# The second gate/up piece of each expert issued by ScalarE on its own queue

## The reference

```python
def swiglu(x, w_gate, w_up, w_down):
    return (jax.nn.silu(x @ w_gate) * (x @ w_up)) @ w_down

yb = swiglu(x_pad[tok], w_gate_e[e], w_up_e[e], w_down_e[e]).astype(jnp.float32) * w[:, None]
```

## Time and profile before

| | us |
|---|---|
| median of three runs | 1398.07 (1396.43 to 1402.14) |
| the profiled execution | 1402.14 |
| its span in the trace | 1400.4 |
| TensorE busy | 1307.5 (93%) |
| TensorE weight load busy | 973.2 (69%) |
| VectorE busy | 900.2 (64%) |
| ScalarE busy | 706.9 (50%) |
| GpSimd busy | 420.8 (30%) |

### The profile page before, as it was taken

How to read it: one execution, slowest core, us unless ns; L and a number is a source line. 1 busy time by engine, 2 the same in 40 slices (tenths; PEclk the granted TensorE clock), 3 DMA queues, 4 the chain that set the end, 5 groups by cost and what they waited for, 6 DMA issues and landing times.

```text
span 1400.4 us, 15961 instructions
## 1 busy us (share of the span) xinstructions
PE 1307.5 (93%) x6084; PEld 973.2 (69%) x6084; DVE 900.2 (64%) x1167; ACT 706.9 (50%) x863; POOL 420.8 (30%) x266
## 2 busy tenths in 40 slices
PE   7999999999979999989799999999999999999865
PEld 4989886666656776455587777777777777777722
DVE  4001116645666565564388888888888888888858
ACT  4222333333323221012377888887888778887610
POOL 3232312212223342017233333323233333233204
PEclk9999999999999999989999999999999999999978
DMA  4732202111112151430499999999999999999684
GB/s 154 259 102 72 68 20 68 64 39 38 57 38 67 65 203 54 195 132 19 155 387 373 372 365 370 374 366 370 362 373 360 361 365 371 361 363 349 233 368 179
DMA packets 75291, 311.36 MB, mean 222 GB/s; under 512 B 17660, under 2 KB 17788, under 8 KB 57040
## 3 DMA queue, kind: packets, MB, share of 16 engines
q1 hardware_dynamic: 55728, 276.64, 53.8%
q0 software_dynamic: 19488, 33.70, 6.4%
HBM read 305.74 MB, written 42.01 MB: 248 GB/s over the span
## 4 chain that ended last, share of the span: by engine, by line
PE 65%; DMA 21%; DVE 4%; ACT 4%; issue 3%; POOL 3%; POOLq 0%; SPq 0%; DVEq 0%; ACTq 0%
DMA raw<-in_w_gu 19%; PE PS L647 18%; PE PS L891 9%; PE PS L841 5%; PE PS L844 4%; PE PS L838 4%; PE PS L755 4%; PE PS L703 4%; PE PS L773 3%; ACT w_hi_e L1109 3%; PE PS L726 3%; POOL tab_d L1628 2%; PE PS L714 2%; PE PS L675 2%; PE PS L676 2%
## 5 line engine op out<-in xcount | busy, mean ns | idle before, releaser
L1426 DVE TENSOR_TENSOR w_lo_e<-raw,w_hi_e 128x2048 fp32r<-128x2048 f32 x192 | 435.3, 2285 | 14.3 <-ACT w_hi_e L1109 14.0
L1109 ACT ACTIVATE w_hi_e<-raw 128x2048 fp32r<-128x2048 f32 x192 | 368.3, 1919 | 119.8 <-DMA raw<-in_w_gu 75.1
L1642 POOL DMA_INDIRECT y_d<-y_slots,tab x64 | 120.8, 1887 | 412.1 <-ACT y_slots L1141 284.7
L1596 POOL TENSOR_TENSOR w_lo<-ring,w_hi 128x1024 fp32r<-128x1024 f32 x54 | 128.3, 2376 | 327.0 <-ACT w_hi L1016 327.0
L1269 DVE CUSTOM_DVE_ANT_0 region<-PS,region 128x128 f32<-128x128 f32 (+1 forms) x64 | 30.6, 478 | 183.2 <-PE PS L703 181.1
L838 PE MATMUL PS<-w_hi_e,xs_hi 128*128 128x512 f32 x512 | 144.2, 403 | 0.0
L841 PE MATMUL PS<-w_hi_e,xs_lo 128*128 128x512 f32 x512 | 142.8, 401 | 0.0
L844 PE MATMUL PS<-w_lo_e,xs_hi 128*128 128x512 f32 x512 | 137.5, 390 | 0.0
L1060 ACT ACTIVATE region<-region,nmax 128x128 f32<-128x128 f32 (+3 forms) x80 | 43.6, 546 | 150.3 <-DVE nmax L1269 150.0
L841 PEld LDWEIGHTS PS<-w_hi_e,xs_lo 128*128 128x128 f32 x512 | 92.7, 188 | 30.6 <-DVE xs_lo L1452 12.4
L844 PEld LDWEIGHTS PS<-w_lo_e,xs_hi 128*128 128x128 f32 x512 | 96.2, 188 | 20.8
(11 more groups left out here) (182 smaller groups left out, 2154.3 us busy)
## 6 DMA issues: line engine op xcount, KB each, us to landing
raw<-in_w_gu SPq DMA_DIRECT2D x128, 1024.0 KB, 11.3
raw<-in_w_down_e SPq DMA_DIRECT2D x64, 1024.0 KB, 11.0
ring<-in_w_merge SPq DMA_DIRECT2D x32, 640.0 KB, 4.0
parts<-y_d SPq DMA_DIRECT2D x8, 1536.0 KB, 16.2
ring<-in_w_proj SPq DMA_DIRECT2D x22, 512.0 KB, 3.7
region<-in_w_out SPq DMA_DIRECT2D x1, 4096.0 KB, 14.1
parts<-y_d SPq DMA_DIRECT2D x4, 1024.0 KB, 19.9
bias_d<-bias_rows SPq DMA_DIRECT2D x3, 1280.0 KB, 11.7
```

The costliest lines, as they stand in the source:

```text
L1109: nc.scalar.activation(w_hi_e[b][:, lo:hi], raw[b][:, lo:hi], ACT.Copy).then_inc(made, 1)
L1426: nc.vector.tensor_tensor(w_lo_e[b][:, lo:hi], raw[b][:, lo:hi], w_hi_e[b][:, lo:hi].bitcast(F32), ALU.subtract).then_inc(made, 1)
L1596: nc.gpsimd.tensor_tensor(wl, w, wh.bitcast(F32), ALU.subtract).then_inc(w_lo_made, 1)
L1642: pool.indirect_dma_start(y_d, bass.IndirectOffsetOnAxis(ap=rows, axis=0), y_slots[:, b, :], None, bounds_check=last_row, oob_is_err=False ...
```

## The change

The second piece of experts 1 to 63 is no longer issued by SyncE (its wait on `gu_b` goes with it) but by ScalarE, on ScalarE's own queue. It has no wait of its own: it stands behind `make_silu`, which waits for the same `gu_b` count. The second piece of expert 0 stays on SyncE.

```diff
             for e in range(1, N_EXP):
                 sp.wait_ge(gu_a, e + QT - 1)
                 load_first(e)
-                sp.wait_ge(gu_b, e + QT - 1)
-                load_second(e)
                 if e >= 2:
                     sp.wait_ge(y_done, e + QT - 2)
                     load_down(e - 1)
...
+            def load_second(e):
+
+                act.dma_start(raw[e % 2][:, PART:GU], a["w_gu"][e][:, PART:GU]).then_inc(p1_in[e % 2], 16)
+
...
             make_silu(3)
+            load_second(1)
             copy_hT(3)
             high_x(0)
             for e in range(N_EXP):
...
                     high_second(e + 1)
                 make_silu(e + QT)
+                if e + 2 < N_EXP:
+                    load_second(e + 2)
                 high_down(e)
```

## The result

The change makes the kernel slower by 1%: 1412.76 us (median of 4 runs, 1409.14 to 1422.03) against 1397.38 us on the same chip, a ratio of 1.0101, 95% interval 1.0073 to 1.0129. 1398 had been predicted. An unchanged copy of the changed kernel gave 1.0087 later (1.0053 to 1.0121), and a copy of the one before 1.0000.

A forecast was written before the change was run, and what follows sets the result against it. It took the transfers, with DMA engines near their end (share 0.98, 367 GB/s), to set the 10.0 us period. All terms were 0, summing to 0 on the profiled 1402.14 us; against the median it forecast 1398 us, range 1391 to 1405.

The forecast's parts named there:

- What bounds the kernel: Experts' loop: transfers at 367 GB/s set the 10.0 us period, TensorE 7% behind; landing time is the line's length.
- Issue work: 63 issues moved from SyncE to ScalarE: covered by its waiting for pieces, taken as 0, at most 21 us.
- The time of the issue: Second piece on ScalarE: issued 3.3 us later behind the silu, landing in 7.8 us, just when needed; 0.
- SyncE's wait: Down weights on SyncE: now wait only for `y_done`, which comes last anyway; 0, at most 3.6 us gained at the start.
- So the rate stays and with it the period.: Transfers in the loop: the line never runs empty, so the period stays at 10.0 us; main term, 0.
- First piece shares and lands later: First piece's landing: second piece takes turns from it, up to 2.0 us at one expert in three; 1418 us, chance 0.20.
- the faster rival: First piece's landing: comes earlier, so TensorE stops less; 13 us gained, 1385 us, at most 43 us; chance 0.24.
- Gathers late: Gathers: a second busy queue slows them to 15.9 us where 15.7 is allowed; 6 us slower or 1428 us; chance 0.06.
- Same line after all: ScalarE's transfers: join the same line, so only the 3.3 us later issue stays; slower, chance 0.04.

The follow-up runs named there:

- spread: The kernel before, with the slots in use put on even and odd partitions alike: ratio 0.9704, 1359.23 us.
- b_early: The changed kernel with the second piece issued ahead of the rounding of the previous second piece, behind its own wait on `gu_b`: ratio 1.0050, run again 1.0040.
- a_half: The changed kernel with the first piece in two transfers with rows of 4 KB instead of one with 8 KB: ratio 1.0210.
- b_half: The changed kernel with the second piece in two transfers with rows of 4 KB instead of one with 8 KB, on ScalarE: ratio 1.0437.
- before_b_half: The kernel before with the second piece in two transfers with rows of 4 KB, on SyncE's one line: ratio 1.0061.
- a_act: The kernel before with the first piece issued by ScalarE on its own queue, the second staying on SyncE: ratio 1.0108.

## Why the prediction was wrong, by its own steps

- **What bounds the kernel.** Right that the transfers set the pace and that the hop from first piece to copy to down product is where TensorE stops: all of its new idle time came there. Wrong that 367 GB/s was an end, and that a landing is the length of one line: the 8th of 16 increments came after 6.4 us, so the long line was that of half of the parts. A mean share of 0.98 over 16 engines does not say that the next order of the same bytes could not go faster: spread moved them at 395. Both had a share near 1, so a share counts time under way, not rate.
- **Issue work, 0.** Nothing in the runs speaks against it: the same small transfer costs the same from SyncE.
- **The time of the issue.** This step failed. It took the place behind the silu for the time of the silu, so 3.3 us later in every period. The sequencer runs ahead, and the median issue is no later than before. In exchange it can be held by any landing that is waited for ahead of it, here in 22 of 62 periods, which the step didn't look at. b_early against the change shows the price: 0.5%. That the second piece would land in 7.8 us was too low also: 9.3 in the median, 10.2 in the expert shown.
- **SyncE's wait, 0.** Right. At the start the down weights of expert 1 did go at 689.66, right behind the first piece of expert 2 (before: 4.0 us behind it); the next first piece followed that of expert 2 by 6.4 us in both kernels, so it brought nothing.
- **"So the rate stays and with it the period."** This is the main term, put at 60 x (10.0 - 10.0) = 0, and it failed: 10.21 us and 360 GB/s, 12.6 us in the loop. The argument was that a line of three or four pieces never runs empty. It does run thin when the piece that is waited for is not the one being moved: TensorE stops, frees no buffer, and nothing new is issued (a share of 0.87 in the expert of 13.82 us). The total in the line doesn't help then, only its order.
- **The rivals.** "First piece shares and lands later" was the right side and place, with 1418 us against 1413, at a chance of 0.20. That its figure is so close is in part luck: it has 20 stalls, each longer by 1 us. Measured were 20 (24 before) of 1.7 us (1.0), 11.5 us more in all, and half of the loss goes with the gate, which this rival lacks. Its picture was too uniform: the median landing became shorter (10.9), as the faster rival had said, and the longest ones longer (15.6). The mean hides this, the maximum and the longest wait show it. "Gathers late": scatters take 10.7 us to land (9.2 before), but TensorE doesn't wait for rows. "Same line after all": q10 excludes it. The Trainium skill's rule that a DMA engine goes round its queues packet by packet (DMA: Bandwidth & Descriptors, Queues, rings and completion order) was cited for the first of these rivals and should have had more weight: 0.75 against 0.54 MB in 4.9 us, in 99 and 95 packets, agrees with it. So do the landing times of a_half and b_half: on two queues the piece with the smaller rows lands later (12.9 against 11.4 us, 11.0 against 9.3), while in one line it doesn't (before_b_half, 11.4 against 11.2).
- The limit of some 358 GB/s for a core (DMA: Bandwidth & Descriptors, Specifications, in the Trainium skill) isn't one here: 395 GB/s over 558 us. The page itself puts it at a core's half when both cores of a pair stream, so for this kernel, which runs on one core, it was no argument against the faster rival.

What stays open: where the 0.4 to 0.5% of b_early comes from. Lost order is one cause, its own wait for `gu_b` another; no run separates them. That half of the engines carried the gathers is inferred from the gain of spread and from the increments, since the profile names no single engine. And a_act: its loop (10.07) explains less than its ratio, and neither its first piece nor its issues are late.

## What to carry to other kernels

A queue is also an order: before a piece is moved to a queue of its own, ask which piece it will overtake, and which engine waits for that one. Read an issue from a computing engine by the waits ahead of it, not by the instructions; where one of these waits is the landing of the piece's own predecessor, the period can't be shorter than the landing time. And when DMA engines look full, first see whether their load is even: spreading rows over partitions gave three times what the change cost.

## What the hardware showed that was not expected

- ScalarE's sequencer issued a transfer 4.2 us before the silu ahead of it executed (1008.35, 1012.51).
- The same transfers with the same mean share (0.98, 1.01) ran at 367 or 395 GB/s, by the partitions that the gathered rows use.
- Half of a 1 MB piece landed in 6.4 us and the rest only by 12.0, while the mean share of the DMA engines was 0.98.
- 62 transfers of 1 KB cost 0.3 to 0.5%; two transfers with rows of 4 KB instead of one with 8 in a third of the weights cost 0.6%, and 8 KB rows instead of 4 in another third give 0.3%.
